# Where a depthwise convolution's steps stand among VectorE's other work in two mixer layers

## The reference, cut to what matters

```python
proj = h @ w_in[l]                       # split: a_q, a_kv, a_gate, d_q, d_kv, b_in, c_in
# branch 0: compressed + selected + window attention, gated by ga
o_cmp = softmax(mask(qa @ k_cmp)) @ v_cmp            # 15 compressed keys
o_a = ga0 * o_cmp + ga1 * o_slc + ga2 * o_win
# branch 1: conformer convolution, 31 taps over 512 channels
c = a * sigmoid(gte)
c = causal_depthwise_conv(c, conv_w, conv_b)
o_b = silu(layer_norm(c, ln_g, ln_b))
# branch 2: pool mixer; branch 3: window attention with sinks
up = einsum("bsnc,ncd->bsnd", [o_a, o_b, o_c, o_d], w_branch)
gates = sigmoid(h @ w_gate)
x = x + rms_norm((sum over branches of gates * up) @ w_o)
# then an FFN with a 3-tap convolution
```

## Time and profile before

| | us |
|---|---|
| median of 3 runs | 1821.84 (1820.89 to 1829.63) |
| the profiled execution | 1830.08, of which the span 1828.0 |
| mean granted TensorE clock | 0.951 |
| TensorE busy in matmuls | 1680.5 (92% of the span) |
| VectorE, ScalarE, GpSimd busy | 1084.7 (59%), 760.2 (42%), 261.6 (14%) |
| layer 0, layer 1, second block | about 0 to 548, 548 to 1091, 1091 to 1828 |

### The profile page before, as it was taken

The page is one execution under the profiler, slowest core; times in us unless marked ns, Lnnn a source line. Parts: engine busy times, 40 slices in busy tenths (PEclk is TensorE's granted clock), DMA queues, the critical chain, the costliest instruction groups (busy, mean ns, idle before and its releaser), DMA issues. The chain is left out here.

```text
span 1828.0 us, 26603 instructions
## 1 busy us (share of the span) xinstructions
PE 1680.5 (92%) x10712; PEld 1383.9 (76%) x10712; DVE 1084.7 (59%) x1490; ACT 760.2 (42%) x1069; POOL 261.6 (14%) x293
## 2 busy tenths in 40 slices
PE   7998997899998989998899989999898978999996
PEld 5887897699977888887799974445475537899995
DVE  4668987566645668987566631284547334454555
ACT  4355654455534355554455422113116224333431
POOL 0200004144301200003144200014320000000000
PEclk9999998899999999998899999999869987999998
DMA  6544454466553545454466554112000232355551
GB/s 252 185 185 162 185 185 151 149 234 250 184 200 139 211 157 184 169 178 158 151 237 224 187 185 170 69 69 91 25 23 1 70 115 93 139 184 184 184 182 70
DMA packets 40121, 282.07 MB, mean 154 GB/s; under 512 B 4816, under 2 KB 5072, under 8 KB 6864
## 3 DMA queue, kind: packets, MB, share of 16 engines
q1 hardware_dynamic: 38432, 273.15, 41.4%
q10 hardware_dynamic: 1584, 7.42, 1.2%
HBM read 279.50 MB, written 1.05 MB: 153 GB/s over the span
## 5 line engine op out<-in xcount | busy, mean ns | idle before, releaser
L428 DVE TENSOR_TENSOR ring_low<-ring,sb_hi 128x2048 fp32r<-128x2048 f32 x116 | 267.9, 2309 | 192.3 <-ACT sb_hi L423 191.9
L423 ACT ACTIVATE sb_hi<-ring 128x2048 fp32r<-128x2048 f32 x116 | 222.5, 1918 | 285.9 <-DMA ring<-weights 114.4
L577 PE MATMUL psum<-sb_hS,sb_hi 128*128 128x256 f32 x704 | 203.3, 289 | 4.8 <-DVE ring_low L428 4.7
L1848 DVE TENSOR_TENSOR sb_split<-ring,sb_split 128x2048 fp32r<-128x2048 f32 x48 | 109.9, 2292 | 153.2 <-ACT sb_split L1843 153.2
L580 PE MATMUL psum<-sb_hS,sb_hi 128*128 128x256 f32 x704 | 200.3, 284 | 0.0
L581 PE MATMUL psum<-sb_hS,ring_low 128*128 128x256 f32 x704 | 199.4, 283 | 0.0
L839 PE MATMUL psum<-sb_hfT,ring_low 128*128 128x256 f32 x704 | 198.1, 281 | 0.0
L2162 PE MATMUL psum<-sb_hfS,sb_split 128*128 128x256 f32 x512 | 146.5, 286 | 6.0 <-DVE sb_hfS L2692 3.9
L2165 PE MATMUL psum<-sb_hfS,sb_split 128*128 128x256 f32 x512 | 145.8, 285 | 0.0
L2166 PE MATMUL psum<-sb_hfS,sb_split 128*128 128x256 f32 x512 | 145.8, 285 | 0.0
L577 PEld LDWEIGHTS psum<-sb_hS,sb_hi 128*128 128x128 f32 x704 | 134.9, 192 | 14.1 <-DVE ring_low L428 7.2
(11 more groups left out here) (392 smaller groups left out, 3881.7 us busy)
## 6 DMA issues: line engine op xcount, KB each, us to landing
ring<-weights SPq DMA_DIRECT2D x256, 1024.0 KB, 4.8
sb_rows_ffn<-rows ACTq DMA_DIRECT2D x4, 512.0 KB, 4.7
sb_rows_mix<-rows ACTq DMA_DIRECT2D x2, 1024.0 KB, 5.0
sb_rows<-rows ACTq DMA_DIRECT2D x1, 2048.0 KB, 9.1
sb_x<-x_in SPq DMA_DIRECT2D x2, 512.0 KB, 5.9
sb_y<-ctx_in SPq DMA_DIRECT2D x1, 1024.0 KB, 6.4
out<-sb_x SPq DMA_DIRECT2D x2, 512.0 KB, 2.7
sb_const<-const SPq DMA_DIRECT2D x1, 711.0 KB, 13.5
```

The costliest lines, as they stand in the source:

```text
L423: act.activation(hi_of(n), ring[:, c % SLOTS, :], ACT.Copy).then_inc(hi_ready, 1)
L428: eng.tensor_tensor(low_of(n), ring[:, SPLIT_CHUNKS[n] % SLOTS, :], hi_of(n).bitcast(F32), ALU.subtract).then_inc(lo_dve, 1)
L577: mm = pe.matmul(out, hi[:, k, bs], hS[:, 0, k, :], start=(k == 0), stop=False)
L1848: dve.tensor_tensor(split[:, n % SPLITS, 1, :], ring[:, (first_moe + n) % SLOTS, :], split[:, n % SPLITS, 0, :].bitcast(F32), ALU.subtract ...
```

## The change

- The compressed part's weighing (`cmp_weigh`) moves on VectorE from behind the low part of pass 1 to ahead of it.
- The conv steps of the seven passes are 4, 18, 16, 10, 10, 12, 20 instead of 12 each.
- In the up stage 4 steps follow each gate product, instead of 3, 5, 3, 5, 3 and the rest; the low part of a chunk follows these steps rather than preceding the 5.
- `CONV_BEFORE` moves the conv's transposes and norm one product ahead, to before up (0,2); `OB_BEFORE` the transposes back to before (3,0) and (3,1).
- GpSimd's roots (`conv_roots`) stand ahead of all its additions of the up stage instead of behind the third.
- ScalarE makes the high part of chunk FIRST_UP + 6 behind both silu parts rather than between them.
- VectorE makes the conv branch's low parts behind product (3,1) and before that chunk's low part, instead of behind product (3,2).

No instruction is added or removed.

```diff
--- before.py
+++ after.py
@@ -283,8 +283,9 @@
             jobs.plan(("down", c, t), ("s0", "s1", "t", "u")[2 * t + c])
 
 
-CONV_BEFORE = (0, 3)
-OB_BEFORE = {(3, 1): 0, (3, 2): 1}
+CONV_BEFORE = (0, 2)
+OB_BEFORE = {(3, 0): 0, (3, 1): 1}
+CONV_STEPS = (4, 18, 16, 10, 10, 12, 20)
 BRANCH_ORDER = (2, 0, 3, 1)
 
 
@@ -1052,8 +1053,6 @@
         for n in range(FIRST_UP + 2, FIRST_UP + 6):
             split_hi(act, n)
         for t in range(TT):
-            if t == 1:
-                split_hi(act, FIRST_UP + 6)
             jobs.wait_filled(act, ("obT", t))
             for b in range(4):
                 jobs.drain(act.activation(acc[:, b, t * P:(t + 1) * P], jobs.out(("obT", t))[:, b * P:(b + 1) * P], ACT.Silu,
@@ -1062,7 +1061,7 @@
             jobs.wait_drained(act, ("up", BRANCH_ORDER[0], 3))
             act.activation(brS[1][:, 0, :, t * P:(t + 1) * P], acc[:, :, t * P:(t + 1) * P], ACT.Copy).then_inc(ob_hi, 1)
         load_rows(act, "post_mix", 2 * D, mem["rows_mix"][:, :, :].rearrange("p i c -> p (i c)"), mix_rows_in)
-        for n in range(FIRST_UP + 7, FIRST_WO + 1):
+        for n in range(FIRST_UP + 6, FIRST_WO + 1):
             split_hi(act, n)
 
         def mix_high(i):
@@ -1372,12 +1371,12 @@
                 mask(r, 1)
             if 2 * r - 1 in TURN_AFTER_GATE:
                 mod_in(TURN_AFTER_GATE[2 * r - 1])
+            if r == 1:
+                cmp_weigh()
             split_lo(dve, FIRST_GATE + 2 * r + 1)
             if r == 0:
                 pool_low()
                 cmp_blocks()
-            if r == 1:
-                cmp_weigh()
             if r >= 2:
                 out_low(r - 2)
             if r < len(ROUNDS):
@@ -1388,7 +1387,7 @@
                 mod_in(TURN_AFTER_GATE[2 * r])
             if r == 0:
                 cmp_mask()
-            conv_steps(12)
+            conv_steps(CONV_STEPS[r])
         split_lo(dve, FIRST_GATE + 15)
         out_low(len(ROUNDS) - 1)
         conv_steps(8)
@@ -1431,19 +1430,17 @@
                 jobs.drain(dve.tensor_tensor(dst, jobs.out(name), g2, ALU.mult), name)
                 if (n, i + 1) == CONV_BEFORE:
                     conv_norm()
-                if (n, i + 1) == (3, 3):
-                    for t in range(TT):
-                        dve.wait_ge(ob_hi, t + 1)
-                        part = brS[1][:, :, :, t * P:(t + 1) * P]
-                        dve.tensor_tensor(part[:, 1, :, :], acc[:, :, t * P:(t + 1) * P], part[:, 0, :, :].bitcast(F32),
-                                          ALU.subtract).then_inc(ob_lo, 1)
-                if i % 2 == 0:
-                    conv_steps(3)
-                else:
+                conv_steps(4)
+                if i % 2 == 1:
                     chunk = 2 * bi + i // 2
+                    if chunk == 4:
+                        for t in range(TT):
+                            dve.wait_ge(ob_hi, t + 1)
+                            part = brS[1][:, :, :, t * P:(t + 1) * P]
+                            dve.tensor_tensor(part[:, 1, :, :], acc[:, :, t * P:(t + 1) * P], part[:, 0, :, :].bitcast(F32),
+                                              ALU.subtract).then_inc(ob_lo, 1)
                     if chunk < 7:
                         split_lo(dve, FIRST_UP + chunk + 2)
-                    conv_steps(5 if chunk < 2 else 4 * TAPS)
                     if chunk == 6:
                         mix_low(0)
                         mix_low(1)
@@ -1565,6 +1562,7 @@
                 pool.tensor_tensor(lnstd[:, t:t + 1], msq[:, 2:3], K("mhalf", 0, 1), ALU.pow).then_inc(lnstd_ready, 1)
                 pool.wait_ge(lnstd_ready, t + 1)
 
+        conv_roots()
         k = 0
         for n in BRANCH_ORDER[1:]:
             for i in range(4):
@@ -1574,8 +1572,6 @@
                 dst = mixT[:, 2 * i:2 * i + 2, :].rearrange("p b t -> p (b t)")
                 pool.tensor_tensor(dst, dst, tmp[:, k % 2, :], ALU.add).then_inc(mixed, 1)
                 k += 1
-                if (n, i + 1) == CONV_BEFORE:
-                    conv_roots()
 
         post_roots(0)
         pre_roots(1)
```

## The result

| | before | changed |
|---|---|---|
| median | 1825.74 us (6 runs, 1818.73 to 1830.31) | 1808.22 us (6 runs, 1803.83 to 1809.64) |
| ratio, 95% interval | | 0.9896 [0.9871, 0.9922] |
| profiled execution | 1830.08 us | 1809.64 us, of which the span 1807.7 |
| median, once more beside the experiments | 1827.82 us (14 runs) | 1809.43 us (4 runs), ratio 0.9906 [0.9874, 0.9938] |

(The ratio is not exactly the quotient of the two medians.) The change is faster by 1.0%, 17.5 us between the medians and 20.4 us between the two profiled executions. Forecast were 1795.0 us and 26.8 us, with 1806 as the upper end. So the direction holds and the size doesn't.

What follows compares the result with a forecast made beforehand. TensorE's waits and half clock were taken to bound the kernel. 6.3 + 8.8 - 1.7 = 13.4 us a layer, 26.8 in both, off the median 1821.84 gave 1795.0 us, range 1785 to 1806.

Steps and rivals of the forecast that it cites:

- What bounds: TensorE is busy 92% of the span; only its waits and slowed clock matter, a ceiling of 20.5 us a layer.
- Part 1: Weighing moved up, 4 steps in round 0: the 6.03 us wait falls to 0.6, a new 1.15 appears; gain 6.9 us.
- Part 2: Conv steps of 4, 18, 16, 10, 10, 12, 20 over the rounds: VectorE's appointments lose TensorE 0.6 us a layer.
- lead after the rounds: TensorE's gain a layer on entering the up stage: 6.9 - 0.6 = 6.3 us, lower bound 3 us.
- sign of being wrong: TensorE's waits for low parts in the rounds adding up to over 2 us a layer would point to VectorE overload.
- rival 2: VectorE is overloaded in rounds 1 and 2: lead 3 instead of 6.3 us, 1801.6 us; chance 0.14.
- Rival 5: The weighing waits for something other than its place on VectorE, so its move brings nothing: 1807.6 us; chance 0.05.
- The 0.4 us late in round 2: Round 2's low part on VectorE ends at 176.3 against 175.9 wanted by TensorE: 0.4 us lost.
- Part 3: Up stage: the 8.24 us wait falls to 2.8, the 1.29 us wait goes; gain 8.8 us a layer before the clock.
- My 0.5 us for GpSimd's additions: Up stage: additions behind the roots collide with a low part, so TensorE waits 0.5 us, bounds 0 and 2.2.
- The clock: Half clock around the 2.8 us wait left in the up stage: a loss of 1.7 us a layer, bounds 0 to 3.4.
- The base: The 26.8 us gain was set against 1821.84 us, the median of the runs shown, giving 1795.0 us.

Runs made afterwards that it cites:

- Filling the wait: Changed kernel with five of round 1's 18 conv steps put ahead of its second low part: 1800.19 us, ratio 0.9853 to the kernel before.
- the kernel without the half clock: Changed kernel with five steps moved into round 1's wait and 18 placed ahead of and in round 0: 1792.06 us, ratio 0.9822 to before.
- the change's rounds alone: The change's weighing place and steps per round, with the up stage of the kernel before: 1814.59 us, ratio 0.9938 to before.

## Why the prediction was wrong, point by point

**What bounds.** Right. TensorE's waits and its clock carried the gain; the second block moved by 0.6 us.

**Part 1.** Right. Waits of 0.67 and 0.9 us against 0.6 and 1.15, the clock at 1.00; 6.7 us gained by the end of gate chunk 3, forecast 6.9.

**Part 2: the step that failed.** I took "weighing of the scores and another low part" as 4.3 us by subtracting the 0.98 us wait for ScalarE in the earlier trace rows and let the low part follow at once, at 143. In the trace of before that wait did hang on TensorE: ScalarE's high part stood behind a copy that waited for the late transposes, and it did go when these came earlier. What I left out is what the high part meets next. Its weights land at 143.0 (143.4 before, by the estimate above), a time set by the end of gate chunk 2 and not by the transposes, so it stayed where it was when TensorE no longer stood still, and VectorE waited 2.16 us. The term "lead after the rounds" was 6.3 us and measured 3.4, of which 1.96 us are the wait and 1.5 us its half clock, less 0.5 that I had counted as lost. Filling the wait gave 3.2 and 3.3 us a layer back in the rounds. Twice 2.9 us are 5.8 of the 6.4 us missing in the profiled pair. My sign of being wrong did show: TensorE's waits for low parts in the rounds add up to 2.9 us a layer, over the 2 that I had named for rival 2. Rival 2 had the right place and nearly the right size (lead 3, 1801.6 us) with the wrong cause: VectorE had enough time for the steps, not in that place. Rival 5's time, 1807.6 us, is the nearest to the measured one, and that is luck: its mechanism did not happen, since the wait for the weighing fell from 6.03 to 0.67 us.

**The 0.4 us late in round 2, the rounds behind it.** Not seen: TensorE had lost more than that by then. The appointments of rounds 3 to 6 were kept.

**Part 3.** The conv transposes waited 2.86 us (2.8), the 1.29 us wait went, the stage gave 7.5 us with the clock (7.1). My 0.5 us for GpSimd's additions didn't appear on TensorE. The collision was there: a low part beside them took 2.76 us and the next 3.00, against 2.2 to 2.3 alone,

```profile
277.78 2.76 DVE L429 TENSOR_TENSOR ring_low<-ring,sb_hi 128x2048 fp32r<-128x2048 f32 x1
...
283.35 3.00 DVE L429 TENSOR_TENSOR ring_low<-ring,sb_hi 128x2048 fp32r<-128x2048 f32 x1 [0.86 <-ACT sb_hi L424]
```

and four additions took 7.10 us:

```profile
277.09 7.10 POOL L1573 TENSOR_TENSOR sb_mixT<-sb_mixT,sb_tmp 128x512 f32<-128x512 f32 x4
```

but TensorE, slowed by the half clock, arrived later still. In the kernel without the half clock, a wait of 0.5 us for this low part is there.

**The clock.** 3.41 us at 0.50 around the 2.86 us wait, 1.5 us, for a term of 1.7.

**The base.** The forecast gain off the profiled execution would have been 1803.3 us, but I set it against the median of the three runs shown, 1821.84. With more runs the median of before was 1825.74, 1827.82 and 1826.59, its runs lying between 1818.7 and 1830.3; three were too few. Of the 13.2 us between 1795.0 and 1808.2, 6.4 are the gain's size in the profiled pair, and the rest is this base and the scatter between executions. My upper end of 1806 had 4 us for all this and nothing for the base. Set against 1825.74 us, the same gain gives 1798.9 us and the same distance an upper end of 1809.9, above the measured 1808.2. A better base alone would so have put the measurement inside the range, with the step in part 2 as wrong as it is.

## What to carry to other kernels

A wait that a change is to remove has to be followed to its origin, and then one step further: what would the same instruction wait for next, once this origin comes earlier? Here that was a transfer's landing. It stayed where it was in time when the engine in front sped up, and the work queued behind it moved with it. So when filler work is put among appointments on an in-order engine, look for the waits there and put it ahead of one rather than behind it. Here five steps of 0.4 us on the other side of one line were worth 6.5 us by the traces (9 by the medians), and more steps in two idle places around round 0 another 7. Take a base from as many runs as the expected gain needs.

## What the runs showed of the hardware

A wait of TensorE of about 2 us is not always paid with the clock. In the changed kernel's first profile 1.96 us in round 2 of layer 0 were followed by a granted clock of 0.50 for 3.41 us; in its second profile the same place had a longer wait and kept 1.00:

```profile
158.88 0.38 PE L578 MATMUL psum<-sb_hS,sb_hi 128*128 128x256 f32 x1 [2.16 <-DVE ring_low L429]
```

```profile
158.90:162.30 3.40, 3.40 (x29) 3.40 (x30) 3.27 (x6) 2.75 (x3) 0.00 (x0) 1.00 0.12 51
```

In layer 1 of the same execution 2.04 us in this place were followed by 3.41 us at 0.50, and in the kernel with the change's rounds alone 1.98 us by 6.83 us at 0.50. Identical programs so differ by such stretches, and whether a wait this long costs 2, 3.5 us or more can't be read from its length. Some of the scatter between executions can be this; how much was not measured apart. Some lies ahead of the stage: the first score product of layer 0 began at 112.82 us in the changed kernel's first profile and at 111.06 in its second.
